# Chunk inverses of the gated delta rule: full 128x128 products, or pairs of 64x64x64 products in two corners of the array

## The reference, cut to what matters

```python
def gated_delta_rule(q, k, v, g, beta):
    ...
    kb = k * beta[..., None]
    a_low = jnp.where(strict, jnp.einsum('bhnid,bhnjd->bhnij', kb, k) * decay, 0.0)
    eye = jnp.eye(c, dtype=q.dtype)
    rhs = jnp.concatenate([v * beta[..., None], kb * jnp.exp(cum)[..., None]], axis=-1)
    sol = lax.linalg.triangular_solve(eye + a_low, rhs, left_side=True, lower=True)
    u, w = sol[..., :dv], sol[..., dv:]
```

## Time and profile before

| what | value |
|---|---|
| time, three runs | 2370.43, 2370.70, 2371.64 us, median 2370.7 us |
| profiled execution | span 2370.3 us; for its own time outside the span nothing is listed |
| PE busy | 2262.8 us (95%) |
| DVE, ACT, POOL busy | 1506.0, 1269.6, 276.4 us |
| the four rounds of inverses | about 916 to 1075 us of the span, 38.0 to 39.3 us each |

### The profile page before, as it was taken

The page is one execution under the profiler, slowest core; times in us unless marked ns, Lnnn a source line. Parts: engine busy times, 40 slices in busy tenths (PEclk is TensorE's granted clock), DMA queues, the critical chain, the costliest instruction groups (busy, mean ns, idle before and its releaser), DMA issues. The chain is left out here.

```text
span 2370.3 us, 29415 instructions
## 1 busy us (share of the span) xinstructions
PE 2262.8 (95%) x11234; PEld 1794.2 (76%) x11234; DVE 1506.0 (64%) x1871; ACT 1269.6 (54%) x1680; POOL 276.4 (12%) x273
## 2 busy tenths in 40 slices
PE   7999999999999999999999999999995999999994
PEld 6878558777777768998888878888774777777773
DVE  3534842569978677656334555355337899988886
ACT  4334541588874436552324423235424888888884
POOL 2000000123320212330000000000001111121210
PEclk9999999999999999999999999999996999999997
DMA  6222103423214433001222212334125999999995
GB/s 232 72 71 89 36 21 112 131 76 100 97 61 139 155 125 125 2 1 54 89 95 94 96 36 81 124 115 160 54 101 227 376 408 409 409 402 401 400 401 193
DMA packets 119817, 377.41 MB, mean 159 GB/s; under 512 B 9608, under 2 KB 38592, under 8 KB 94496
## 3 DMA queue, kind: packets, MB, share of 16 engines
q1 hardware_dynamic: 106432, 332.49, 38.0%
q0 software_dynamic: 12768, 37.13, 4.7%
q10 hardware_dynamic: 512, 6.34, 0.6%
HBM read 363.02 MB, written 21.02 MB: 162 GB/s over the span
## 5 line engine op out<-in xcount | busy, mean ns | idle before, releaser
L2270 DVE TENSOR_TENSOR w_lo<-raw,w_hi 128x2048 fp32r<-128x2048 f32 x117 | 267.9, 2290 | 460.0 <-ACT w_hi L1618 459.7
L1618 ACT ACTIVATE w_hi<-raw 128x2048 fp32r<-128x2048 f32 x117 | 223.8, 1913 | 407.5 <-PE bank L863 368.6
L863 PE MATMUL bank<-hT_hi,w_hi 128*128 128x512 f32 x512 | 201.6, 394 | 4.6 <-DVE hT_lo L2334 2.3
L863 PE MATMUL bank<-hT_hi,w_lo 128*128 128x512 f32 x512 | 200.6, 392 | 0.0
L863 PE MATMUL bank<-hT_lo,w_hi 128*128 128x512 f32 x512 | 200.5, 392 | 0.0
L1072 PE MATMUL bank<-hT_hi,w_hi 128*128 128x512 f32 x432 | 173.8, 402 | 0.9 <-DVE hT_lo L2334 0.9
L1072 PE MATMUL bank<-hT_hi,w_lo 128*128 128x512 f32 x432 | 168.2, 389 | 0.0
L1072 PE MATMUL bank<-hT_lo,w_hi 128*128 128x512 f32 x432 | 168.1, 389 | 0.0
L3106 DVE TENSOR_TENSOR e_lo<-eraw,e_hi 128x2048 fp32r<-128x2048 f32 x62 | 141.9, 2290 | 36.1 <-ACT e_hi L2150 36.0
L2990 DVE TENSOR_TENSOR e_lo<-raw,e_hi 128x2048 fp32r<-128x2048 f32 x64 | 146.6, 2291 | 8.2 <-ACT e_hi L2133 7.9
L2990 DVE TENSOR_TENSOR w_lo<-raw,w_hi 128x2048 fp32r<-128x2048 f32 x64 | 144.2, 2286 | 8.9 <-ACT w_hi L2133 8.8
(11 more groups left out here) (590 smaller groups left out, 5344.0 us busy)
## 6 DMA issues: line engine op xcount, KB each, us to landing
raw<-expert_w_gate SPq DMA_DIRECT2D x64, 1024.0 KB, 11.1
raw<-expert_w_up SPq DMA_DIRECT2D x64, 1024.0 KB, 11.6
eraw<-expert_w_down SPq DMA_DIRECT2D x64, 1024.0 KB, 10.8
raw<-w_in SPq DMA_DIRECT2D x40, 1024.0 KB, 5.1
raw<-even_w_in SPq DMA_DIRECT2D x18, 1024.0 KB, 5.3
raw<-odd_w_in SPq DMA_DIRECT2D x16, 1024.0 KB, 5.4
raw<-even_w_out SPq DMA_DIRECT2D x8, 1024.0 KB, 5.1
raw<-odd_w_out SPq DMA_DIRECT2D x8, 1024.0 KB, 5.1
```

The lines of the kernel that those rows point to most:

```text
L863: mm = pe.matmul(out, st, mv, start=first and x == 0, stop=last and x == 2)
L1618: act.activation(split_to(m)[0][:], raw[n % RAW][:], ACT.Copy).then_inc(sem("hi_done"), 1)
L2270: dve.tensor_tensor(split_to(m)[1][:], raw[split_of[m] % RAW][:], f32(split_to(m)[0][:]), ALU.subtract).then_inc(sem("lo_done"), 1)
```

## The change

The inverses of the 64x64 diagonal blocks are computed as such. The 128x128 system of a chunk has two of them, upper left (`UP`, partitions 0 to 63) and lower right (`LOW`, 64 to 127). In the changed kernel their matrices lie one above the other in tiles of 128 partitions x 64 columns. Each former product of 128x128x128 is two products of 64x64x64, one in rows and columns 0 to 63 of the array, one in rows and columns 64 to 127. Only the last level, the block below both, is done by itself at full chunk: its product with the block and a transposed inverse go to partitions 0 to 63, and one more product follows. Transposes on 64x64 blocks are products with the identity. The tiles copied and added by ACT and DVE have half the columns. POOL's masks act on two 64-partition halves each. k and v scaled for the right-hand sides go to tiles of their own.

```diff
+HF = P // 2
+UP, LOW = slice(0, HF), slice(HF, P)
+HALVES = (UP, LOW)
...
         def part(e, dst, level):
-            return pool.tensor_tensor(dst, gs[e][2][:], m_level[level].unsqueeze(1).to_broadcast([P, 2, P]), ALU.mult)
+            for r in HALVES:
+                ins = pool.tensor_tensor(dst[r], gs[e][2][r, :, r], m_level[level][r].unsqueeze(1).to_broadcast([HF, 2, HF]), ALU.mult)
+            return ins
...
+        def blocks(e, b, at, f, inc=None):
+            for c in range(2):
+                for r in HALVES:
+                    mm = pe.matmul(bank(e, b)[r, at + c * HF:at + c * HF + HF], *f(c, r), start=True, stop=True)
+            if inc:
+                mm.then_inc(sem(inc), 1)
...
-                two(e, 0, 0, lambda c: (nm16[e][:, 1, c], nm16[e][:, 0, c]))
-                two(e, 0, 256, lambda c: (nm16[e][:, 0, c], nm16[e][:, 1, c]), "g_2pe")
+                blocks(e, 0, 0, lambda c, r: (nm16[e][r, 1, c], nm16[e][r, 0, c]))
+                blocks(e, 0, P, lambda c, r: (nm16[e][r, 0, c], nm16[e][r, 1, c]), "g_2pe")
...
-            for lv in range(3):
+            for lv in range(2):
                 for e in EE:
-                    two_T(e, 0, 0, lambda c: gs[e][7][:, c])
-                    two(e, 0, 256, lambda c: (o[:, c], gs[e][7][:, c]), f"g_TYpe{lv}")
+                    blocks(e, 0, 0, lambda c, r: (g_R[e][r, c], ident[r, r]))
+                    blocks(e, 0, P, lambda c, r: (below[e][r, lv, c], g_R[e][r, c]), f"g_TYpe{lv}")
                 for e in EE:
                     pe.wait_ge(sem(f"g_TY{lv}"), n + e + 1)
-                    two(e, 1, 0, lambda c: (nm2[e][:, 0, c], nm2[e][:, 1, c]), f"g_Jpe{lv}")
+                    blocks(e, 1, 0, lambda c, r: (nm2[e][r, 0, c], nm2[e][r, 1, c]), f"g_Jpe{lv}")
+            for e in EE:
+                pe.wait_ge(sem("g_J1"), 2 * (n + e) + 2)
+                for c in range(2):
+                    pe.matmul(bank(e, 0)[UP, c * HF:c * HF + HF], gs[e][7][UP, c, UP], ident[UP, UP], start=True, stop=True)
+                    mm = pe.matmul(bank(e, 1)[UP, c * HF:c * HF + HF], gs[e][2][LOW, c, UP], gs[e][7][LOW, c, LOW],
+                                   start=True, stop=True)
+                mm.then_inc(sem("g_TYpe2"), 1)
+            for e in EE:
+                pe.wait_ge(sem("g_TY2"), n + e + 1)
+                pe.wait_ge(sem("g_Y2"), n + e + 1)
+                for c in range(2):
+                    mm = pe.matmul(bank(e, 1)[UP, c * HF:c * HF + HF], nm2[e][UP, 0, c], nm2[e][UP, 1, c], start=True, stop=True)
+                mm.then_inc(sem("g_Jpe2"), 1)
```

More of the change, by code:

```diff
@@ L90, in constants @@
         np.where(i > j, 0.0, BIG),
[L91 to L94, removed]
+        np.concatenate([in_half(same(16)), in_half(same(32) & ~same(16))], 1),
+        np.concatenate([in_half(same(64) & ~same(32)), in_half(i == j)], 1),
         (i <= j) & same(QC),
@@ L224, in view @@
         return nc.alloc_sbuf_tensor_at(name, shape, dtype, offset=regions + region * REG + at)
-    masks = place("masks", [P, 13, P])
+    masks = place("masks", [P, 11, P])
     ident, m_le, m_gt, m_addT, m_addS = (masks[:, k] for k in range(5))
-    m_level = [masks[:, k] for k in (5, 6, 7, 8)]
-    m_hgrn, m_before, ones, iota = (masks[:, k] for k in (9, 10, 11, 12))
+    m_level = [masks[:, 5, 0:HF], masks[:, 5, HF:], masks[:, 6, 0:HF]]
+    ident_half = masks[:, 6, HF:]
+    m_hgrn, m_before, ones, iota = (masks[:, k] for k in (7, 8, 9, 10))
     rope_at = cursor[0]
@@ L756, in _ @@
                 part(e, nm16[e][:, 1], 0).then_inc(sem("g_M16"), 1)
+            if n == 0:
+                for e in range(4):
+                    pool.memset(gs[e][7][LOW, :, UP], 0.0).then_inc(sem("g_zero"), 1)
+                pool.wait_ge(sem("g_zero"), 4)
+            pool.wait_ge(sem("g_M16"), n + 4)
             for e in range(4):
@@ L762, in _ @@
                 pool.tensor_tensor(q, q, gs[e][0][:], ALU.mult).then_inc(sem("g_qdec"), 1)
-                pool.wait_ge(sem("g_qdec"), n + e + 1)
-                part(e, gs[e][0][:], 1).then_inc(sem("g_M32"), 1)
+            pool.wait_ge(sem("g_qdec"), n + 4)
             for e in range(4):
[L766 to L770, removed]
+                if n:
+                    pool.wait_ge(sem("g_TYpe1"), n + e - 3)
+                part(e, below[e][:, 0], 1).then_inc(sem("g_M32"), 1)
+                part(e, below[e][:, 1], 2).then_inc(sem("g_M64"), 1)
         together(pool, 13)
@@ L1983, in _ @@
                 act.wait_ge(sem("g_2pe"), n + e + 1)
-                act.activation(nm2[e][:], gbank(e, 0, 0, 512), ACT.Copy).then_inc(sem("g_2"), 1)
+                act.activation(nm2[e][:], halves(e, 0, 0, 2 * P), ACT.Copy).then_inc(sem("g_2"), 1)
             if n == 0:
@@ L1996, in _ @@
                 hi_to(m + 14)
-            for lv in range(3):
+            for lv in range(2):
                 for e in EE:
                     act.wait_ge(sem(f"g_TYpe{lv}"), n + e + 1)
-                    act.activation(nm2[e][:], gbank(e, 0, 0, 512), ACT.Copy).then_inc(sem(f"g_TY{lv}"), 1)
+                    act.activation(nm2[e][:], halves(e, 0, 0, 2 * P), ACT.Copy).then_inc(sem(f"g_TY{lv}"), 1)
                 if lv == 1 and n + 4 < 2 * HEADS:
                     decay_rows(n + 4, EE)
+            for e in EE:
+                act.wait_ge(sem("g_TYpe2"), n + e + 1)
+                act.activation(nm2[e][UP, 0], halves(e, 0, 0, P, UP), ACT.Copy).then_inc(sem("g_TY2"), 1)
+            for e in EE:
+                act.wait_ge(sem("g_Jpe2"), n + e + 1)
+                act.activation(gs[e][7][UP, :, LOW], halves(e, 1, 0, P, UP), ACT.Copy).then_inc(sem("g_J2"), 1)
             if n + 4 < 2 * HEADS:
@@ L2797, in _ @@
             grow("g_Jpe0", 1, "g_J0")
-            grow("g_Jpe1", 1, "g_J1")
+            for e in EE:
+                dve.wait_ge(sem("g_Jpe1"), n + e + 1)
+                dve.wait_ge(sem("g_zero"), e + 1)
+                for r in HALVES:
+                    dve.tensor_tensor(gs[e][7][r, :, r], halves(e, 1, r=r), g_R[e][r], ALU.add).then_inc(sem("g_J1"), 1)
+            for e in EE:
+                dve.wait_ge(sem("g_TYpe2"), n + e + 1)
+                dve.tensor_copy(nm2[e][UP, 1], halves(e, 1, r=UP)).then_inc(sem("g_Y2"), 1)
             if n + 4 < 2 * HEADS:
                 differences(n + 4, EE, 2, m_addS, "g_D")
-            grow("g_Jpe2", 1, "g_J2")
-            if n + 4 < 2 * HEADS:
                 differences(n + 4, EE, 1, m_addT, "g_DT")
```

65 lines of the change are left out of this document (38 added, 27 removed).

## The result

The changed kernel takes 2338.29 us (median of 4 runs, 2337.95 to 2340.06), the kernel before 2370.56 in the same comparison: ratio 0.9862, 95% interval 0.985 to 0.9874. I had predicted 2330 us, with 2321 to 2362 as the range. 32.3 us were won and not 40.3, so a fifth of the forecast gain is missing.

What follows compares the result with a forecast made beforehand. PE bounds the rounds, with DVE's queue nearly as long in the tail. A round of 39.3 us becomes 17.4 + 10.3 = 27.7; three rounds win 34.8, the first 5.5, together 40.3: 2370.3 becomes 2330 us, range 2321 to 2362.

Steps and rivals of the forecast that it cites:

- A record of 64x64x64: PE in the rounds: 0.028 us each with two corners at once, 528 records in place of 256.
- Rival (1): PE's corners take turns, 0.056 us a record, four rounds +4 us, 2375 us; chance 0.08.
- Rival (2): PE cannot start records so densely, 0.067 us each, +5.8 us a round, 2393 us; chance 0.06.
- The round trips: Front, PE through ACT or DVE and back: mostly covered, 0.7 us a round with the change of array shape.
- the front: Gram products to the second level's first sum, PE alone decides: 26.7 us becomes 17.4, 9.3 won.
- Rival (4): Round trips show in full, 5 to 8 us a round more, 2351 to 2362 us; chance 0.08.
- POOL in the front: POOL's masks, each now two of about 450 ns: costs nothing to 1 us a round, taken as nothing.
- The tail: Second level's first sum to last u and w product, DVE's queue: 12.6 us becomes 10.3, 2.3 won.
- the eight half sums: DVE at the start of the tail: 0.20 us each, 1.6 us together.
- The wait of 1.4 us for g_vB: PE in the tail waits for DVE's scaled k and v: about 1.4 us, up from 1.2.
- The first round: Wins less than the 11.6 us of the others, since ACT, DVE and POOL finish other work: 5.5 us.
- Rival (3): PE's clock falls: short drops 2338 us, down through the rounds 2403; chance 0.06, 0.04 of it short drops.

Runs made afterwards that it cites:

- upper_twice: Changed kernel with the alternating 64x64x64 products of the upper corner issued twice, the lower ones once; 2377.11 us, ratio 1.002.
- levels_first: Changed kernel with POOL's masks of `below` for both levels moved ahead of the products of qkvT; 2331.44 us, ratio 0.9829.
- fused_masks: Changed kernel, POOL's order kept, both levels' masks of a half in one instruction of 256 columns; 2333.35 us, ratio 0.984.
- dt_late: Changed kernel with DVE's four differences for `g_DT` moved behind the scalings of k and v; 2334.69 us, ratio 0.9844.

## Why the prediction came out as it did

**A record of 64x64x64: right.** 0.028 us taken, 0.029 measured, and by upper_twice for the reason given, two corners at once. Rival (1) is out. The Trainium skill's rule for it (TensorEngine Tiling (Array Packing), Restrictions and Gotchas: different row tiles cannot access the same PSUM bank at once) does not hold here: both corners write one bank, on other partitions of it, alternately, at 0.029 us a record. Rival (2) is out by the same rows: 80 starts in 2.33 us are below its 0.067 us. They are below the 62 ns per MATMUL too that the Trainium skill names (TensorE: Matmul & The Clock Gate, "Wait — 56ns, not 53.3ns?").

**The round trips: right, and the number in part by luck.** Without POOL's waits the front is 19.6 - 2.2 = 17.4 us, the number predicted. But 456 records at 0.029 are 13.3 us where I had 12.8, and about 0.3 is left for round trips and changes of shape, for which I had put 0.7. Rival (4) did not occur.

**POOL in the front: wrong.** The step that failed is "It costs nothing to 1 us a round; I take nothing". It cost 2.17 us in each of rounds two to four. Half masks were priced by columns, at 0.42 to 0.45 us (450 ns is the duration of one), but come every 0.51 us, so 24 of them take 12.3 us and not 10.3; the last pair's mask was ready 14.4 us after POOL's start and not at 12.5, and PE wanted it at 12.4. The prediction's own figures warned of it: 3.5 + 3.3 + 14/16 of 6.8 is 12.75 us and not 12.5, and with every half mask at its 450 ns it is 13.2, 1.2 us behind PE's 12. A margin of half a microsecond on a queue of 28 instructions was no margin; levels_first and fused_masks show that this was the whole loss in the front.

**The tail: mechanism right, a size wrong.** The term is the eight half sums, 1.6 us at 0.20. They take 2.53, 0.32 each, nearly the 0.33 at which the instructions of 256 columns come. That is 0.93 of the 1.0 us missing; it is read from DVE's queue, which has no gap there, and no run takes this term away by itself. The wait of 1.4 us for g_vB came as forecast. The 0.20 was right for other forms: in DVE's timeline the next instruction starts 0.20 us behind a whole sum of 128 columns,

```profile
986.85 0.29 DVE L2839 TENSOR_TENSOR g_R<-bank,g_R 128x128 f32<-128x128 f32 x1 [0.20 <-PE bank L1200]
987.05 0.41 DVE L2842 TENSOR_TENSOR intraT<-bank,gs 128x256 f32<-128x256 f32 x1
```

and the four copies of 128 columns on 64 partitions (1001.62 above) come every 0.20 as well ((0.88 - 0.28) / 3). So half the partitions cost as much as all, and the half sums, which go to the upper and the lower partitions by turns, cost 0.12 more each. The masks on POOL show the same: 0.51 from start to start at 0.45 long, where whole ones came every 0.69 at 0.73 long. On both engines the next instruction began before the last had ended where both lay in the same partitions, and after it where they lay in opposite halves. No run separates this from the other differences in form (what is read and written with gaps), so the cause is not shown.

**The first round: 1.4 us better than predicted**, by offsetting parts, which is luck: ACT's work showed less, since POOL held PE up in its place (levels_first uncovers it), and one fall of the clock cost about 1.7 us.

**The clock.** Rival (3) happened once in four rounds, behind a stretch in which PE was busy 1.76 of 4.00 us:

```profile
928.00:932.00 4.00, 1.76 (x53) 1.55 (x51) 0.64 (x2) 3.99 (x5) 3.46 (x9) 1.00 0.00 0
932.00:935.40 3.40, 3.40 (x70) 3.40 (x68) 2.75 (x5) 0.85 (x4) 2.69 (x2) 0.51 0.14 18
...
961.30:964.40 3.10, 1.32 (x38) 1.11 (x36) 0.00 (x0) 1.15 (x3) 2.70 (x7) 1.00 0.00 0
```

In the rounds behind it the clock stayed up through nearly the same waits (the last row is round two), and in dt_late it did not. What decides it stays open.

**Sum.** 9.8 us missing in rounds two to four (6.5 POOL, 2.8 half sums, 0.5 not assigned), 1.4 too much in the first: 8.3 of stage, against 8.0 by the medians. In the fourth round, which has no differences and no wait for g_vB, the share of the half sums is taken over from the others and not read. The range held because it had room for an error of this size, 1 us a round for POOL and half sums at 0.26.

## What to carry to other kernels

When the engine that bounds a stage gets faster, take every queue that feeds it through the stage by the pace of its instructions (span over count), not by the duration of one, and count a margin under a microsecond as none. Work split by partitions cost nothing on PE, where two corners run at once, and full price and more on POOL and DVE (two half masks 1.02 us for one of 0.69, two half sums 0.63 for one of 0.20); look there for the new bound. Cheap reordering (masks ahead of products that nobody waits for, differences behind scalings, another part's weight unit a round later) was then worth 13 us of the stage (140.9 to 127.7, some 1.7 of it the clock) with no change in what is computed.

## What was not expected of the hardware

- Two products of 64x64x64 in opposite corners run at once into one bank, 0.029 us a record on average, and a record occupies its corner for 0.058; sixteen, eight for one corner and then eight for the other, take 0.58 and not 0.47 us.
- POOL: 256 columns on 64 partitions 723 ns, every 0.79 us, on 128 partitions 733 ns, every 0.69 us; 128 columns on 64 partitions 451 ns, every 0.51 us.
- DVE: behind a sum of 128 columns on 128 partitions the next instruction starts 0.20 us on, copies of 128 columns on 64 partitions come every 0.20, and sums on 64 partitions, alternating between the halves, every 0.32. (The whole sums at 996.26 come every 0.23, which is how PE delivers them: eight records at 0.029.) Why the half sums are slower was not tried.
- PE's clock was at 1.2 GHz for 3.4 or about 7 us behind the three stretches shown (PE busy 1.76 of 4.00, 1.62 of 3.40 and 1.47 of 4.20 us), with half of that time lost at most; behind one with PE busy 1.32 of 3.10 us it stayed at 2.4 GHz. No single wait in the first of these was longer than 1.39 us.
